# Latent attention: one bank for q's two sums of squares, and another split of the k and v phase over ScalarE, VectorE and Pool

## What is computed

```python
q = (rms_norm(c_q, q_norm_g) @ w_qb).reshape(B, S, H, MLA_QK_DIM)      # 8 heads, 128 + 64
kv = (rms_norm(c_kv, kv_norm_g) @ w_kvb).reshape(B, S, H, 128 + 128)
k_nope, v = kv[..., :128], kv[..., 128:]
k = jnp.concatenate([k_nope, k_rope], axis=-1)                         # k_rope shared by the heads
q = rms_norm(q, q_head_g)                                              # over the 192 of a head
k = rms_norm(k, k_head_g)
# rotary step on the last 64 of q and k, then block-causal softmax attention, 2048 frames
```

## Time and profile before

| | us |
|---|---|
| median of 3 runs | 4075.6 (4072.52 to 4077.5) |
| the profiled execution | 4080.59 |
| its span, core 2, the slowest | 4079.6 |
| spans of the eight cores | 4057.6 to 4079.6 |

### The profile page before, as it was taken

The page is one execution under the profiler, slowest core; times in us unless marked ns, Lnnn a source line. Parts: engine busy times, 40 slices in busy tenths (PEclk is TensorE's granted clock), DMA queues, the critical chain, the costliest instruction groups (busy, mean ns, idle before and its releaser), DMA issues.

```text
span 4079.6 us, 62233 instructions; the slowest of 8 cores (4057.6 to 4079.6 us)
## 1 busy us (share of the span) xinstructions
PE 3846.2 (94%) x20843; PEld 1921.3 (47%) x21232; DVE 2096.5 (51%) x3814; ACT 1610.6 (39%) x2538; POOL 664.8 (16%) x746
## 2 busy tenths in 40 slices
PE   6999999999988889999999999999999898889999
PEld 3455554444435454444454554544444454544444
DVE  4444437737354446727534445475473544467272
ACT  2433334313257574403233332542232666644130
POOL 1233221010011011110023234110000111200000
PEclk8999999999999999999999999999999999999999
DMA  6222123454321111665451231243533201214643
GB/s 152 43 56 56 27 41 50 73 91 70 66 59 32 22 35 24 97 134 109 99 126 27 49 67 24 43 68 64 91 61 68 51 27 27 53 32 77 130 72 84
DMA packets 92469, 262.77 MB, mean 64 GB/s; under 512 B 8704, under 2 KB 9856, under 8 KB 92160
## 3 DMA queue, kind: packets, MB, share of 16 engines
q0 software_dynamic: 57824, 184.84, 27.4%
q1 hardware_dynamic: 34336, 73.93, 5.7%
HBM read 426.77 MB, written 16.78 MB: 109 GB/s over the span
## 4 chain that ended last, share of the span: by engine, by line
PE 86%; ACT 4%; issue 4%; DVE 3%; DMA 2%; POOL 1%; SPq 0%; ACTq 0%; DVEq 0%; POOLq 0%
PE psum L365 83%; PE psum L1119 2%; ACT m_P L368 2%; DMA ring<-wts 1%; DVE hT L374 1%; POOL r_u L378 1%; DMA xT<-xin 1%; ACT m_sqq L368 1%; ACT m_rsq L368 1%; ACT n_sq L368 0%; DVE m_ot L371 0%; DVE m_kn L381 0%; SPq L243 0%; DVE xT L371 0%; DVE r_P L374 0%
## 5 line engine op out<-in xcount | busy, mean ns | idle before, releaser
L365 PE MATMUL psum<-hT,ring 128*128 128x512 bf16 x7915 | 1784.6, 382 | 47.2 <-DMA ring<-wts 17.9
L365 PEld LDWEIGHTS psum<-hT,ring 128*128 128x128 bf16 x8064 | 788.9, 98 | 1007.2 <-issue 77.8
L371 DVE TENSOR_TENSOR xT<-xT,psum 128x512 f32<-128x512 f32 x512 | 350.3, 686 | 688.9 <-PE psum L365 667.4
L368 ACT ACTIVATE f_c<-psum,prm_s 128x512 f32<-128x512 f32 x352 | 273.3, 777 | 1036.0 <-PE psum L365 1025.2
L374 DVE SCALAR_TENSOR_TENSOR f_c<-psum,prm_s,f_c 128x511 f32<-128x511 f32 x704 | 526.8, 748 | 258.2 <-ACT f_c L368 209.1
L365 PE MATMUL psum<-f_uT,ring 128*128 128x512 bf16 x2766 | 607.5, 379 | 2.6
L243 POOL DMA_DIRECT2D ring<-wts x390 | 208.4, 541 | 2059.1 <-PE psum L365 1955.7
L368 ACT ACTIVATE m_P<-psum,m_rstdk 128x512 bf16<-128x512 f32 (+3 forms) x640 | 386.0, 626 | 137.7 <-PE psum L1119 128.4
L365 PEld LDWEIGHTS psum<-f_uT,ring 128*128 128x128 bf16 x2816 | 274.9, 98 | 332.8
L365 PE MATMUL psum<-r_u,ring 128*128 128x512 bf16 x976 | 242.9, 379 | 6.8 <-DVE xT L371 2.6
L1119 PE MATMUL psum<-m_v,m_P 128*128 128x129 bf16 x2176 | 234.9, 221 | 13.9 <-DVE m_ot L371 12.3
(11 more groups left out here) (111 smaller groups left out, 3103.4 us busy)
## 6 DMA issues: line engine op xcount, KB each, us to landing
ring<-wts POOLq DMA_DIRECT2D x250, 512.0 KB, 7.4
ring<-wts POOLq DMA_DIRECT2D x128, 352.0 KB, 4.5
m_rope<-mrope SPq DMA_DIRECT2D x40, 512.0 KB, 4.2
xT<-xin SPq DMA_DIRECT2D x32, 512.0 KB, 15.6
r_rt<-rrope SPq DMA_DIRECT2D x32, 512.0 KB, 3.8
xout<-xT SPq DMA_DIRECT2D x32, 512.0 KB, 7.2
ring<-wts POOLq DMA_DIRECT2D x4, 1024.0 KB, 11.5
ring<-wts POOLq DMA_DIRECT2D x8, 288.0 KB, 4.2
```

The lines of the kernel that those rows point to most:

```text
L365: return kb.op('pe', lambda e: e.matmul(out, lhsT, rhs, start=start, stop=stop), reads, writes, signal)
L368: return kb.op('act', lambda e: e.activation(out=out, in_=in_, func=func, **kw), reads, writes)
L371: return kb.op('dve', lambda e: e.tensor_tensor(out=out, in0=a, in1=b, op=op), reads, writes)
```

## The change

**q chain.** The sums of both heads go into one bank: rows 0 to 63 hold head 0's sum and rows 64 to 127 head 1's. The stationary matrices are new: `halves[:, a, :]` has ones in the 64 columns of head a, `blocks` is block diagonal with ones; `halfa` and `halfb` are gone. That takes three matmuls in place of four, one Ln and one Exp (into `rstd`, a tile used elsewhere for other norms), and one `scale_r` over all 128 rows. The scaling of the plain parts needs each head's value on all rows: four DMAs on SP's queue copy the 64-row halves of `rstd` into `m_rsq`, issued behind the Exp. `scale_n` becomes two stages and moves behind `turn`. A chain now has 12 stages.

**k and v phase.** All v copies are ScalarE's. Pool squares every second k block (i even and below 13), ScalarE the others. `m_sqk` has five slots in place of three, and its sums are issued three iterations later. The buffers of `m_ot`, whose place `m_sqk` now reaches into, are set up after each k and v phase.

**Start.** The loaded table has 512 columns in place of 768, and `halves` and `blocks` are written by six memsets of VectorE.

```diff
@@ -316,8 +316,8 @@
         negmb = sb("negmb", [128, 128], BF16)
-        halfa = sb("halfa", [128, 128], BF16)
-        halfb = sb("halfb", [128, 128], BF16)
+        halves = sb("halves", [128, 2, 128], BF16)
+        blocks = sb("blocks", [128, 128], BF16)
         rotb = sb("rotb", [128, 128], BF16)
@@ -331,6 +331,12 @@
         kb.op('dve', lambda e: e.memset(ones[:], 1.0), writes=[onesb])
+        kb.op('dve', lambda e: e.memset(halves[:], 0.0), writes=[onesb])
+        kb.op('dve', lambda e: e.memset(blocks[:], 0.0), writes=[onesb])
+        for a in range(2):
+            r = slice(64 * a, 64 * a + 64)
+            kb.op('dve', lambda e, a=a, r=r: e.memset(halves[:, a, r], 1.0), writes=[onesb])
+            kb.op('dve', lambda e, r=r: e.memset(blocks[r, r], 1.0), writes=[onesb])
 
@@ -817,7 +823,7 @@
-            sqk = ar.tensor("m_sqk", [128, 3, 512], BF16, 99.5)
+            sqk = ar.tensor("m_sqk", [128, 5, 512], BF16, 99.5)
@@ -864,7 +870,7 @@
-                    MM(pr[:, b:b + 1], sqkr[:, b * 128:(b + 1) * 128], halfa[:, 0:1], True, True, [sqkrb, constb], [prb],
+                    MM(pr[:, b:b + 1], sqkr[:, b * 128:(b + 1) * 128], blocks[:, 0:1], True, True, [sqkrb, onesb], [prb],
@@ -905,8 +911,11 @@
-            rsqb = [ar.buf('m_rsq%d' % a, 36 + 2 * a, 2) for a in range(2)]
-            otb = [ar.buf('m_ot%d' % i, 102.5 + i, 1) for i in range(2)]
+            rsqa = [ar.buf('m_rsq%d' % a, 36 + 2 * a, 2) for a in range(2)]
+            rsqh = [[Buf('m_rsqh%d%d' % (a, r)) for r in range(2)] for a in range(2)]
+            for a in range(2):
+                for r in range(2):
+                    kb.handoff(rsqh[a][r], [rsqa[a]])
@@ -939,45 +948,52 @@
 
-                def sums(a):
+                def sums():
                     bi = rots(); held.insert(0, bi)
                     ps, psb = bank(bi)
-                    MM(ps, ones[:], sqq[:, a, :], True, False, [sqqb[a], onesb], [psb], signal=False)
-                    MM(ps, (halfa, halfb)[a][:], sqq[:, 2, :], False, True, [sqrb, constb], [psb])
+                    for a in range(2):
+                        MM(ps, halves[:, a, :], sqq[:, a, :], a == 0, False, [sqqb[a], onesb], [psb], signal=False)
+                    MM(ps, blocks[:], sqq[:, 2, :], False, True, [sqrb, onesb], [psb])
 
...
                         held.remove(bi)
-                        ACT(rsq[:, a, :], ps, AF.Ln, [psb], [rsqb[a]], bias=EPS, scale=1.0 / 192)
+                        ACT(rstd[:], ps, AF.Ln, [psb], [rstdb], bias=EPS, scale=1.0 / 192)
                     later.append(log)
 
-                def root(a):
-                    later.append(lambda: ACT(rsq[:, a, :], rsq[:, a, :], AF.Exp, [rsqb[a]], [rsqb[a]], scale=-0.5))
+                def root():
+                    def fn():
+                        ACT(rstd[:], rstd[:], AF.Exp, [rstdb], [rstdb], scale=-0.5)
+                        for a in range(2):
+                            for r in range(2):
+                                kb.dma('sp', 'rs%d%d' % (a, r), rsq[64 * r:64 * r + 64, a, :], rstd[64 * a:64 * a + 64, :],
+                                       reads=[rstdb], writes=[rsqh[a][r]])
+                    later.append(fn)
 
                 def scale_r():
-                    for a in range(2):
-                        r = slice(a * 64, a * 64 + 64)
-                        STT(xg0[r, :], psum[r, 7, :], prm[r, P_QHR:P_QHR + 1], rsq[r, a, :], ALU.mult, ALU.mult,
-                            [pb[7], prmb, rsqb[a]], [xgb[0]])
-
-                def scale_n():
-                    for a in range(2):
-                        STT(Qn[:, s, a, :], psum[:, 5 + a, :], gqk[:], rsq[:, a, :], ALU.mult, ALU.mult,
-                            [pb[5 + a], gqkb, rsqb[a]], [qnb[s][a]])
+                    STT(xg0[:], psum[:, 7, :], prm[:, P_QHR:P_QHR + 1], rstd[:], ALU.mult, ALU.mult,
+                        [pb[7], prmb, rstdb], [xgb[0]])
+
+                def scale_n(a):
+                    STT(Qn[:, s, a, :], psum[:, 5 + a, :], gqk[:], rsq[:, a, :], ALU.mult, ALU.mult,
+                        [pb[5 + a], gqkb] + rsqh[a], [qnb[s][a]])
 
...
                 def rope():
-                    PTT(rsq[:, 0, :], xg0[:], mrope[:, 0, :], ALU.mult, [xgb[0], mropeb], [rsqb[0]])
-                    TT(rsq[:, 1, :], psum[:, 7, :], mrope[:, 1, :], ALU.mult, [pb[7], mropeb], [rsqb[1]])
-                    PTT(Qr[:, s, :], rsq[:, 0, :], rsq[:, 1, :], ALU.add, rsqb, [qrb[s]])
+                    PTT(rsq[:, 0, :], xg0[:], mrope[:, 0, :], ALU.mult, [xgb[0], mropeb], rsqh[0])
+                    TT(rsq[:, 1, :], psum[:, 7, :], mrope[:, 1, :], ALU.mult, [pb[7], mropeb], rsqh[1])
+                    PTT(Qr[:, s, :], rsq[:, 0, :], rsq[:, 1, :], ALU.add, rsqh[0] + rsqh[1], [qrb[s]])
                     made[0] = n + 1
                     if n == 15:
+                        for a in range(2):
+                            for r in range(2):
+                                kb.handoff(rsqa[a], [rsqh[a][r]])
                         ring_i[0] += 7
...
                 none = lambda: None
-                stages.extend([project, lambda: square(0), lambda: square(1), lambda: sums(0), lambda: sums(1), lambda: root(0), lambda: root(1),
-                               none, scale_r, scale_n, turn, none, rope])
+                stages.extend([project, lambda: square(0), lambda: square(1), sums, root, none, scale_r, turn, none,
+                               lambda: scale_n(0), lambda: scale_n(1), rope])
 
@@ -1008,7 +1024,7 @@
                 pssk, psskb = bank(1)
-                sqkb = [ar.buf('m_sqk%d' % i, 99.5 + i, 1) for i in range(3)]
+                sqkb = [ar.buf('m_sqk%d' % i, 99.5 + i, 1) for i in range(5)]
                 begun = []
@@ -1043,12 +1059,9 @@
                     pv4 = pv.rearrange("p (a b) -> p a b", a=4)
-                    if i % 2:
-                        ACT(Vt[:, i, :, 0:128], pv4, AF.Copy, [pvb], [vb[i]])
-                    else:
-                        COPY(Vt[:, i, :, 0:128], pv4, [pvb], [vb[i]])
-                    k = i % 3
-                    if i % 4 == 1:
+                    ACT(Vt[:, i, :, 0:128], pv4, AF.Copy, [pvb], [vb[i]])
+                    k = i % 5
+                    if i % 2 == 0 and i < 13:
                         PTT(sqk[:, k, :], KnT[:, hl, ts], KnT[:, hl, ts], ALU.mult, [knb[hl][tt]], [sqkb[k]])
@@ -1059,9 +1072,10 @@
                     prev.append(tiny)
-                    if i > 1:
+                    if i > 2:
                         prev.pop(0)()
-                prev.pop(0)(); prev.pop(0)()
+                while prev:
+                    prev.pop(0)()
                 TT(rstdk[:], pssk[:, 0:64].rearrange("p (a b) -> p a b", b=4),
@@ -1138,6 +1152,7 @@
                 Pb = [ar.buf('m_P%d' % i, 99.5 + i, 1) for i in range(3)]
+                otb = [ar.buf('m_ot%d' % i, 102.5 + i, 1) for i in range(2)]
                 wos = wload('mo%d' % G, slot(5), 2)
@@ -1174,15 +1189,15 @@
 
-        miscf = ar.tensor("miscf", [128, 768], F32, 100); miscb = ar.buf('misc', 100, 3)
-        kb.dma('sp', 'misc', miscf[:], misc_d, writes=[miscb])
+        miscf = ar.tensor("miscf", [128, 512], F32, 100); miscb = ar.buf('misc', 100, 2)
+        kb.dma('sp', 'misc', miscf[:], misc_d[:, 0:512], writes=[miscb])
         for j in range(4):
...
             x_load(0, 1, j)
-        for dst, c0 in ((identb, 256), (negmb, 384), (rotb, 128), (halfa, 512), (halfb, 640)):
+        for dst, c0 in ((identb, 256), (negmb, 384), (rotb, 128)):
             COPY(dst[:], miscf[:, c0:c0 + 128], [miscb], [constb])
```

## The result

The changed kernel takes 4063.2 us (median; the kernel before on the same chip 4076.8). The ratio is **0.9959, interval 0.9944 to 0.9973**, which is 16.7 us less (11 to 23 by the interval; the two medians lie 13.6 apart); 35 less was forecast. The time lies in the forecast's range, at its slow end, but the gain is half of the forecast's. In some executions the cores of one half of the chip run at a lower granted clock for much of the time; the ratios are of executions without that, and the parts of cores without it.

The account below looks back on a forecast made before the run. VectorE was taken to bound the k and v phase, TensorE the softmax stretch, with ScalarE overtaking at times. Stretches -23, phases -15, copies +3 make -35 us: 4080.6 - 35 = 4045.6, less 5, is 4041; range 4022 to 4066.

Parts of the forecast that it names:

- The lag model of the stretch: Softmax stretch: ScalarE's lag behind TensorE, counted step by step, peaks at 1.25 instead of 1.85 us; -0.82 a chain, -23 us.
- the single sum: Softmax stretch: three matmuls take TensorE 1.31 us against ScalarE's 0.57, lowering ScalarE's lag by 0.7 us.
- The step that failed: q chain: 12 stages instead of 13, with each projection, square and rotation keeping its engine; no cost charged.
- signs against itself: Signs of being wrong: TensorE waiting for m_v or m_sqk, VectorE idle before m_qn over 1 us, longer m_ot waits.
- The sign for it: Softmax stretch: 5 to 6 us shorter, TensorE's waits for m_P and m_rsq nearer 6 than 11 us.
- The copies: Four transfers a chain on SP's queue, landing 2.8 and 3.6 us after the Exp; 0.1 us a chain, +3 us.
- A: Rival: copies land slowly, at Pool's 4.6 us, delaying VectorE and bank releases; 4064 us, chance 0.12.
- B: Rival: slower than before, the same wait with copies landing above 5.0 us; 4099 at 5.7 us, chance 0.05.
- The k and v phase: k and v phases: VectorE's freed work removes TensorE's waits; 3.4 us for G = 0, 4.0 for G = 1, -15 us.
- ScalarE's burst at the chain's head: k and v phase: 13 ScalarE operations in the chain's first five iterations build 1 us of lag; charged 0.7 us.
- hidden in the phases: k and v phase: the Exp ends about 4.5 iterations before m_qn, so the copies cost nothing there.
- C: Rival: waits return through the single sum's TensorE block and an unabsorbed ScalarE burst in the phases; 4062 us, chance 0.13.

Follow-up runs that it names:

- e10: Kernel before, with the second sum, Ln and Exp left out and both heads scaled by the first head's value, stages in their old places; 4047.2 us, one time.
- e19: e10 with a third matmul in the one sum, reading head 0's square, long since there; 4049.9 us, one time.
- e16: e10 with a third matmul in the one sum, reading head 1's square, issued in the step before; 4054.2 us, one time.
- e17: Changed kernel without the four copies, its stages put where the kernel before has them; 4043.3 us, one time.
- e3: Changed kernel without the four copies of a chain, m_qn reading rstd itself; 4050.6 us, ratio 0.9922 to the kernel before.
- e15: Changed kernel with the Ln a step later, an empty step moved ahead of the rotation, and no copies; 4048.8 us, one time.
- e1: Kernel before with only the k and v part of the change; ratio 0.9953 to the kernel before.
- e14: Changed kernel, copies included, with the Ln a step later and the empty step moved ahead of the rotation; softmax stretch G = 0 164.4 us.
- e8: Changed kernel with one empty step moved from behind the rotation to between m_xg and the rotation; eight attention parts sum to 818.0 us.
- e2: Changed kernel with the k and v part taken back, only the q chain's change left; ratio 0.9963 to the kernel before.
- e18: Changed kernel, copies included, with an empty step behind the sum and one between m_xg and the rotation; eight attention parts sum to 818.9 us.

## Why the prediction was right or wrong, point by point

**The lag model of the stretch: right in size, wrong in its floor.** It gave 160.6 for e10, measured 160.8. It took the single sum, 1.31 us of TensorE, as 0.7 us of lag paid back, with nothing of the chain on ScalarE in that step. But the deferred square of head 1 is in it, and the sum waits for it: +0.9 us a stretch (e19 against e16), and the idle 0.53 us before the Ln. Without copies 161.9 was forecast, and 162.7 to 162.8 is what one bank gives in the old places (e17).

**The step that failed** is "A chain has 12 stages instead of 13, but each projection, square and rotation keeps its engine": costed at nothing. The engines stay, but the steps don't: the sum, the root and the rotation move against the reciprocals and m_ot on VectorE and against the exponentials on ScalarE. e3 against e17 puts 2.7 us on it in the stretch of G = 0 and 12.4 us in the eight parts, 8.6 at full clock, the largest miss either way. That the places cost this is shown; how it is spread over the single moves is shown only as far as e15 goes. Two of the prediction's signs against itself are there: m_ot above before's (6.4 against 4.5), and VectorE idle before m_qn for over 1 us (2.15 below). The sign for it, waits for m_P and the logarithm nearer 6 than 11 us, is there too (7.7), and its stretches still weren't 5 us shorter.

**The copies: the right rows, a third of the price.** They land as the row of SP's queue said, and not as Pool's (the median; the slowest took 5.1 us):

```profile
m_rsq<-rstd SPq DMA_DIRECT2D x128, 128.0 KB, 2.3
```

So rivals A and B fall. But the issue was read from one transfer by itself (0.39 us); here four are issued in a row (min/median/max ns):

```profile
L243 SPq DMA_DIRECT2D m_rsq<-rstd x128: 461/594/1725, 1187.5 to 3513.9; - x128
```

On a chain (SP's queue, then the two scalings on VectorE):

```profile
1208.42 2.39 SPq L243 DMA_DIRECT2D m_rsq<-rstd  x4
...
1211.36 0.75 DVE L380 SCALAR_TENSOR_TENSOR m_qn<-psum,m_gqk,m_rsq 128x512 bf16<-128x512 f32 x1 [2.15 <-DMA m_rsq<-rstd]
...
1212.61 0.75 DVE L380 SCALAR_TENSOR_TENSOR m_qn<-psum,m_gqk,m_rsq 128x512 bf16<-128x512 f32 x1 [0.50 <-DMA m_rsq<-rstd]
```

Four issues take 2.39 us and not 1.6. The Exp ends at 1208.3, the first pair is there at 1211.4, 3.1 us on, and the second at 1212.6, 4.3 us on; 2.8 and 3.6 were forecast. VectorE waits 6.3 us for them in the stretch, 0.9 a chain and not "some tenths", and what it costs is 9.4 us (8.1 at full clock), not 3. The estimate from the Trainium skill, "DMA: Bandwidth & Descriptors", section "Anatomy of one DMA" (2.3 us, for the Pool path), agrees with the 2.3 of the row. It is a figure of the landing; part of the cost lay in four issues in a row on SP's queue, for which that section has no figure.

**The k and v phase: the mechanism right, 10.5 instead of 15, and some 13 at equal clock.** k matmuls stand 0.96 us apart (1186.11, 1187.07, 1188.04), as expected. ScalarE's burst at the chain's head, charged 0.7 us, shows as expected, TensorE waiting for a square:

```profile
1183.85 0.38 PE L371 MATMUL psum<-m_sqq,halves 128*128 128x512 bf16 x1 [0.21 <-ACT m_sqq L374]
...
1184.71 0.38 PE L371 MATMUL psum<-m_sqq,halves 128*128 128x512 bf16 x1 [0.49 <-ACT m_sqq L374]
```

In G = 0 the term was 3.4 and measured 3.1 and 3.0. In G = 1 4.0 was forecast, and the medians give 2.5 and 1.9. Most of what is missing is the clock: before has 32.9 with 1.00 in the phase of the first sequence, and the four cores of after with 1.00 have 29.3, 29.3, 29.4 and 29.9, so 3.1 to 3.6 less; its other cores have 0.94 or 0.95 and 31.0 to 32.3. In the second sequence all cores of after have 0.94, and all but one of before's 1.00. TensorE's waits of over 0.15 us in this phase fell from 5.2 to 2.3 us. The prediction called the copies hidden in the phases, and they nearly are: e3, without them, has 29.3 to 29.4 at a clock of 1.00. The 1.27 us of the row of 1395.32 above are core 6's alone.

**The clock.** The half-speed pieces in the phase and stretch of G = 1 weren't in the prediction. The one right behind the phase is gone on all cores of e1 and e17; on nearly all of before, after, e3 and e14 it is there, in e8, e10, e2 and e18 on some. Over all parts they cost 3.4 us in e1, 8.5 in before and 11.9 in after, by the estimate above. What decides it, no run isolates.

**Summed up.** Forecast for the eight parts -35, measured -13.0. The 22 between them are, as measured, 12.4 for the places (e3 against e17), 6.4 for the copies (9.4 against 3), and 3.2 that e17 also lacks (without copies -38 was forecast, it gained 835.4 - 800.6 = 34.8). With the clock taken out it is 8.6 for the places, 5.1 for the copies, 5.5 that e17 lacks, and 2.8 for the clock, which is lower in after than in before; of the 5.5 the square's wait, 0.9 in each of four stretches, is the part that was shown. The split holds for this order of taking things away: in e14's places the copies cost only 3.2. The time, 4063.2, is near two rivals by number. A (4064) has it from copies landing after 4.6 us, and they landed after 2.3. Of C (4062) one half, the single sum as a block, is there but costs 0.9 us a stretch; its other, a burst that isn't absorbed in the phases, isn't: most of the phases' gain came. That the time fell inside the range was luck in part: its slow end came from A and C, and the largest miss, the places, was in neither.

## What to carry to other kernels

In a loop written out in steps, a stage's place is a cost of its own: price each moved stage by what stands in each engine's queue at the new step, before pricing the work saved. To see what a saving is worth, first leave the work out with everything else in its place; if that gives the forecast, the loss lies in the moves. A lag that one engine pays back can't go below zero, so count idle time in both engines, step by step. And before adding up parts of different kernels, set their granted clocks side by side: here a lower clock took 3 to 13 us of these sums, and made two halves of a change look as if they did the same work.
